# One constant of a hybrid decoder step on one core: the sample's threshold search starts 25 head steps earlier

## The reference, cut to what matters

```python
sc = indexer_scores(iq, iw, ik_all)           # (8, 8, 1024 + 8) for the sample
sc = jnp.where(adm[None], sc, -jnp.inf)
_, idx = lax.top_k(sc, topk)                  # topk = 256
...
att = dsa_sample(q, k, v, iq, ik, iw, cache_k, cache_v, cache_ik, page_table, j)
os_ = (att * jax.nn.silu(z)) @ w_out_b[j]
```

## Time and profile before

| | us |
|---|---|
| median of 3 runs (lowest, highest) | 2216.26 (2215.18, 2216.39) |
| the profiled execution | 2213.05 |
| its span in the profile | 2211.3 |
| PE busy | 1999.7 (90%) |
| DVE busy | 999.0 (45%) |
| ACT busy | 685.4 (31%) |
| POOL busy | 599.5 (27%) |

### The profile page before, as it was taken

How to read it: one execution, slowest core, us unless ns; L and a number is a source line. 1 busy time by engine, 2 the same in 40 slices (tenths; PEclk the granted TensorE clock), 3 DMA queues, 4 the chain that set the end, 5 groups by cost and what they waited for, 6 DMA issues and landing times. The chain is left out here.

```text
span 2211.3 us, 33798 instructions
## 1 busy us (share of the span) xinstructions
PE 1999.7 (90%) x12572; PEld 1804.8 (82%) x12572; DVE 999.0 (45%) x1842; ACT 685.4 (31%) x929; POOL 599.5 (27%) x321
## 2 busy tenths in 40 slices
PE   7999998999999999996898888899688988879998
PEld 6999998999999999996763588899455655569898
DVE  3123333111134421424578676789799811231533
ACT  4233332112433332322455222231444532110310
POOL 4333333453333446354110011111100100025221
PEclk8999999999999999997998899999899987789999
DMA  6222222222222233211211203122200014341021
GB/s 167 77 68 76 76 76 76 67 80 83 75 86 85 85 86 86 78 38 49 101 39 26 67 20 88 29 69 79 87 1 1 1 45 154 113 149 47 29 69 41
DMA packets 240516, 152.88 MB, mean 69 GB/s; under 512 B 24946, under 2 KB 235634, under 8 KB 240050
## 3 DMA queue, kind: packets, MB, share of 16 engines
q1 hardware_dynamic: 229314, 140.74, 21.7%
q10 hardware_dynamic: 10192, 9.46, 1.3%
q0 software_dynamic: 928, 1.62, 0.3%
HBM read 135.33 MB, written 16.43 MB: 69 GB/s over the span
## 5 line engine op out<-in xcount | busy, mean ns | idle before, releaser
L392 POOL TENSOR_TENSOR wlo<-wraw,whi 128x1024 fp32r<-128x1024 f32 x177 | 430.5, 2433 | 921.6 <-ACT whi L387 919.9
L404 PE MATMUL PS<-hhi_g,whi 128*128 128x288 f32 (+1 forms) x1536 | 328.3, 295 | 15.3 <-POOL wlo L392 11.1
L404 PE MATMUL PS<-hhi_g,wlo 128*128 128x288 f32 (+1 forms) x1536 | 320.7, 290 | 0.0
L404 PE MATMUL PS<-hlo_g,whi 128*128 128x288 f32 (+1 forms) x1536 | 320.4, 290 | 0.0
L404 PE MATMUL PS<-hhi,whi 128*128 128x364 f32 x1176 | 274.4, 342 | 40.3 <-DVE hlo L1616 12.8
L387 ACT ACTIVATE whi<-wraw 128x1024 fp32r<-128x1024 f32 x177 | 186.6, 1055 | 348.8 <-PE PS L404 310.8
L404 PE MATMUL PS<-hlo,whi 128*128 128x364 f32 x1176 | 265.8, 335 | 0.0
L404 PE MATMUL PS<-hhi,wlo 128*128 128x364 f32 x1176 | 264.6, 334 | 0.0
L404 PEld LDWEIGHTS PS<-hhi_g,whi 128*128 128x128 f32 x1536 | 243.5, 191 | 18.7 <-issue 11.0
L404 PEld LDWEIGHTS PS<-hhi,whi 128*128 128x128 f32 x1176 | 207.0, 194 | 49.6 <-issue 31.7
L404 PEld LDWEIGHTS PS<-hlo_g,whi 128*128 128x128 f32 x1536 | 244.6, 191 | 0.0
(11 more groups left out here) (331 smaller groups left out, 2768.0 us busy)
## 6 DMA issues: line engine op xcount, KB each, us to landing
wraw<-in_w_in_a_dram SPq DMA_DIRECT2D x96, 512.0 KB, 3.9
wraw<-in_w_out_a_dram SPq DMA_DIRECT2D x32, 512.0 KB, 4.1
wraw<-in_w_in_b_dram SPq DMA_DIRECT2D x25, 512.0 KB, 3.8
wraw<-in_w_pe_gate_dram SPq DMA_DIRECT2D x16, 512.0 KB, 4.1
kpg<-in_cache_k_dram SPq DMA_DIRECT2D x64, 128.0 KB, 2.1
vpg<-in_cache_v_dram SPq DMA_DIRECT2D x64, 128.0 KB, 2.0
xs<-xT SPq DMA_DIRECT2D x1, 4368.0 KB, 12.6
xT<-xs SPq DMA_DIRECT2D x1, 4368.0 KB, 13.5
```

The source lines that it names most:

```text
L392: nc.gpsimd.tensor_tensor(wlo[par][:], wraw[par][:], whi[par][:].bitcast(F32), ALU.subtract).then_inc(w_lo, 1)
L404: mm = nc.tensor.matmul(o, w[par][:, k, :], r(k, c0, cn), start=first and i == 0 and n == 0, stop=last and i == KD - 1 and n == 2)
```

## The change

One constant: `SIDE` goes from 25 to 0.

```diff
         BITS, EARLY_BITS, KV_BITS = 31, 8, 2
-        SIDE = 25
+        SIDE = 0
```

## The result

The changed kernel takes 2242.79 us (median of 4; 2235.28 to 2243.84), the kernel before 2215.72 (median of 4 with the runs on the same chip). The medians differ by 27.1 us; the ratio of the means is 1.0117, its 95% interval 1.0093 to 1.0140, which is 26 us slower, between 21 and 31. The profiled execution took 2235.28 us, 22.2 more than the one of before. The forecast was 2242 us.

What follows compares the result with a forecast made beforehand. PE and the hand-over pace the early steps, DVE is full in steps 32 to 57, PE paces block 7. +48.6 up to step 32 and -22.3 behind give +26.3 us on 2216.26: 2242 us, range 2232 to 2252.

Steps and rivals of the forecast that it cites:

- The first part: Stage up to the mask of step 32: 25 search bits moved there outlast DVE's idle time, +48.6 us.
- The `rdiag` term: Searches in iterations 12 and 20: first operation slowed while POOL makes `rdiag`, 0.5 us each, 1.0 us.
- gaps between operations: Steps 0 to 26: 26 gaps of about 0.07 us between masks and what follows, 1.8 us.
- The second part: Mask of step 32 to the stage's end: 128.9 us in place of 151.2, 22.3 us come back.
- The list of PE's work: From step 32's mask: logits 42.4, transposes 22.9, products 46.7 and sums 7.7, together 119.7 us.
- bubbles and stall: From step 32 on: 5.4 us of bubbles, 2.2 at the very end, and 3.0 us where DVE holds PE up.
- PE's sum: Block 5: PE needs 27.6 us against 24.1 us of DVE, so PE sets the pace.
- The repeated writes: 25 added mask writes of 0.75 us, 18.8 us of DVE, cost nothing as long as PE is the limit.
- The clock: Rival: PE's clock falls in blocks 0 to 3, PE limits block 3; +5 us, 2247 us; chance 0.14.
- the prediction's strict reading: PE in blocks 0 to 3: idleness brings the clock throttle back, giving the clock rival its whole price, +5 us.
- DVE past block 4: Rival: resolve parts and repeated writes keep DVE the limit past block 4; +30 us, 2246 us; chance 0.12.
- Not slower: Rival: PE's work is no limit in blocks 4 to 7; -5 us, 2211 us; chance 0.03.

Runs made afterwards that it cites:

- e3: Changed kernel with the sample's counts over 544 of the 1088 columns: median 2222.93 us.
- e2: Changed kernel without the 25 repeated mask writes of the sample: median 2236.91 us, stage 243.79 us.
- e8: Changed kernel without the 25 repeated mask writes, timed a second time: median 2239.35 us, against 2238.53 for the changed kernel.
- e1: Changed kernel timed again with no edit: median 2242.13 us against 2212.05 for the kernel before on that chip, ratio 1.0138.
- e7: Changed kernel timed once more with no edit, beside the one without repeated mask writes: median 2238.53 us.
- e6: Against the kernel before, the sample's 31 bits spread by PE's room, resolve behind the last mask: median 2188.31 us against 2211.44, ratio 0.9898.

## Why the prediction was right

**The first part** was +48.6 us forecast and +47.4 measured (114.77 against 67.33 up to step 32). One bit is 2.30 us after as before, and e3 shows that this DVE time sets the pace. The `rdiag` term was there, and larger than taken: the search's first operation took 0.88 us in iterations 12 and 20, and 0.26 in iteration 16, 1.6 us together where 1.0 was put. Against that, three stalls of the same kind that the kernel before has at line 1530 in blocks 0, 1 and 2 (0.91, 0.41 and 0.28 us in place of 0.16) are gone, 1.1 us that the forecast had counted as DVE's work. What is left of the 1.2 us, about 0.6, is in the gaps between operations, an estimate of 0.07 us per step that came out lower. Iteration 12:

```profile
1604.40 0.59 DVE L1449 SCALAR_TENSOR_TENSOR kTb<-sc,thr,kTb 128x384 f32<-128x384 f32 x1
1605.03 0.88 DVE L1412 TENSOR_TENSOR cand<-tbit,bitc 64x1 uint32<-64x1 uint32 x1
1605.94 0.15 DVE L1413 TENSOR_TENSOR thr<-cand,sgn 64x1 f32<-64x1 f32 x1
```

**The second part** was forecast at 128.9 us and is 128.96. That fits better than its terms deserve. The list of PE's work was right: it makes 120 matmuls of logits, 208 transposes, 216 products and 18 of sums, 562 as in the window. But PE's rows are busy 123.1 us, where the forecast had 119.7 and 0.8, and idle 5.8, where it had 8.4 of bubbles and stall. The work was put about 2.6 us too low and the idle time as much too high. Of the idle time 1.4 us is the one wait for a mask (3.0 forecast), and 2.1 stand behind the last mask, as the 2.2 forecast.

Block 4 took 24.6 us, as its DVE load had said (24.7 forecast; DVE is busy 23.8 of it). Block 5 took 26.2 us and not the 27.6 of PE's sum, but DVE's load is not the reason. Without the repeats (second line, e2) DVE has 6.3 us less to do there, and the block is only 0.1 us shorter; PE is nearly full both times:

```profile
1702.38:1728.58 26.20, 25.70 (x119) 18.31 (x118) 23.21 (x45) 15.60 (x35) 2.90 (x2) 1.00 0.00 1
...
1704.37:1730.47 26.10, 25.60 (x118) 18.21 (x117) 16.93 (x37) 15.45 (x35) 2.90 (x2) 1.00 0.00 1
```

So PE sets the pace from block 5 on. That its work between these two masks is less than the block's own fits the masks' lead over PE's transposes and products, which leaves part of a block's work behind the first mask of the next; no run isolates this.

**The repeated writes** were forecast as hidden. The stage is no shorter without them (e2), and e8 shows no difference in the times. They do collide with `rdiag`, as the prediction said they might: two of them took 1.44 us in place of 0.72, and a part of the sample's resolve in block 4 (line 1447) 2.00 in place of the 1.34 of the earlier trace rows. One of them beside its `rdiag` (timelines of POOL and of DVE):

```profile
1750.70 1.99 POOL L770 TENSOR_TENSOR rdiag<-ident,ars 128x512 f32<-128x512 f32 x1 [14.87 <-DVE ars L1536]
...
1751.83 1.44 DVE L1452 TENSOR_SCALAR scs<-acc 64x1088 bf16<-64x1088 f32 x1
```

**The rivals.** The clock did fall, further than rows of before could show: it was 1.2 GHz almost all through block 0 and in most of block 1. It cost nothing: in e3, with granted clocks of 0.54 and 0.75 in these blocks, they became shorter by all of DVE's saving, so PE's steps still fitted into DVE's. From block 2 on it was mostly at 2.4 GHz again (0.94 and 0.95), though PE was busy only 20.3 of 31 and 23.9 of 33 us. So the +5 us, priced on all of block 3 at 1.2 GHz, did not come, and the prediction's strict reading, by which idle time gives this rival its whole price, does not hold in these rows. Windows of 20, 32, 31, 33 us, blocks 0 to 3:

```profile
1562.00:1582.00 20.00, 13.46 (x32) 7.26 (x32) 18.12 (x74) 6.31 (x24) 1.05 (x1) 0.54 0.43 120
1582.00:1614.00 32.00, 22.19 (x50) 11.15 (x50) 29.37 (x109) 8.77 (x26) 2.36 (x2) 0.63 0.02 5
1614.00:1645.00 31.00, 20.26 (x66) 10.41 (x66) 28.79 (x94) 10.48 (x26) 2.50 (x2) 0.94 0.00 0
1645.00:1678.00 33.00, 23.91 (x86) 13.57 (x86) 30.75 (x95) 12.20 (x26) 2.63 (x2) 0.95 0.00 1
```

DVE past block 4 did not hold PE up. "Not slower" needed a second part under 102.6 us; PE alone is busy 123.1 us there.

**The whole time.** The stage gives +25.2 us; the median moved by 27.1 and in e1's chip by 30.1, in e7's by 26.7. What the profiled executions of the changed kernel differ by, up to 7 us, lies outside the stage, in unchanged code. Over the changed kernel and the eight runs the median moved by -0.4 to +4.9 us more than the stage did, in eight of nine cases upwards; the stage of the kernel before was profiled once, and where those microseconds lie in the executions without a profile is not shown. That the forecast of 2242 met the median to 1 us is partly luck of the same size.

## What to carry to other kernels

Filler work on a second engine is free only where the first engine's step is longer than the second's step plus the filler. Compare them step by step before moving it: growing steps, as in causal attention, want the filler late and in proportion to their room, and a filler put at the front of short steps costs nearly its full length (here 57.5 us of it cost 47.4). In e6 the room of several blocks counted together, and not that of each step, once the steps were long; in the short steps of blocks 1 and 2 a bit still cost 0.9 us on average. A tail in which the second engine waits for the last result is room too.

## What the runs showed that was not expected

- PE's granted clock stood at 0.54 in block 0, where it was 0.97 to 1.00 in the kernel before from 1570 us on, although PE's records are busy for 13.5 of the 20 us. The stage did not get longer by it.
- Several of DVE's operations are drawn out while POOL makes `rdiag`, and not only those with two SBUF inputs: the tiny L1412 from 0.14 to 0.88 us, the running sum over 1088 columns from 2.38 to 3.14 us in e6, and the writing of the mask (L1452), which has one input, from 0.72 to 1.44 us.
- The stage repeats to 0.05 us in three profiles of the changed kernel (243.73, 243.75, 243.78), while the rest of the same program differs by up to 7 us between them.
